# A two-block transformer kernel on one core: where the weight splits stand at the ends of the mixers and of the feed-forward layers

## The reference

```
for layer in range(2):
    u = rms_norm(h, g_mix[layer])
    h = h + mixer(u)                     # layer 0: MLA 8 heads | stick-breaking 8 heads; layer 1: chunk-band, 16 heads
    u = rms_norm(h, g_ffn[layer])
    h = h + (silu(u @ w_gate) * (u @ w_up)) @ w_down          # 1024 -> 2816 -> 1024
x = rms_norm(h, g_final)
```

## Time and profile before

| | |
|---|---|
| median of 3 runs | 1011.17 us (1009.79 to 1012.47) |
| the profiled execution | 1009.69 us |
| its span, first to last instruction | 1007.9 us |
| TensorE busy | 984.0 us, 98% of the span |
| VectorE, ScalarE busy | 629.4 us and 594.7 us |
| granted TensorE clock, mean | 0.998 of full speed |
| chain that ended last | TensorE 91%, ScalarE 4%, VectorE 4% |

### The profile page before, as it was taken

The page is one execution under the profiler, slowest core; times in us unless marked ns, Lnnn a source line. Parts: engine busy times, 40 slices in busy tenths (PEclk is TensorE's granted clock), DMA queues, the critical chain, the costliest instruction groups (busy, mean ns, idle before and its releaser), DMA issues.

```text
span 1007.9 us, 13330 instructions
## 1 busy us (share of the span) xinstructions
PE 984.0 (98%) x4920; PEld 791.8 (79%) x4920; DVE 629.4 (62%) x782; ACT 594.7 (59%) x929; POOL 12.2 (1%) x22
## 2 busy tenths in 40 slices
PE   6999899999999999999999999999999998999998
PEld 5888688888887777788888887877777777778877
DVE  5676675555556765665555556866666666776654
ACT  6776564444445655465454545766767676867571
POOL 1000000000000000000000000000000000000000
PEclk9999999999999999999999999999999999999999
DMA  8536247756563543457757654646434334336551
GB/s 272 177 114 204 84 137 239 247 169 206 168 206 128 180 155 125 127 168 254 227 188 227 231 185 132 207 163 199 132 125 134 116 126 135 118 124 209 197 179 42
DMA packets 106041, 170.26 MB, mean 169 GB/s; under 512 B 3988, under 2 KB 65302, under 8 KB 106000
## 3 DMA queue, kind: packets, MB, share of 16 engines
q1 hardware_dynamic: 103360, 161.23, 48.6%
q0 software_dynamic: 2304, 8.37, 2.6%
q10 hardware_dynamic: 336, 0.10, 0.0%
HBM read 168.58 MB, written 1.11 MB: 168 GB/s over the span
## 4 chain that ended last, share of the span: by engine, by line
PE 91%; ACT 4%; DVE 4%; issue 1%; DMA 0%; ACTq 0%; DVEq 0%
PE acc L434 13%; PE acc L436 12%; PE acc L435 12%; PE acc L485 11%; PE pair_ps L436 7%; PE pair_ps L434 7%; PE pair_ps L435 7%; PE acc L536 3%; PE acc L713 3%; PE acc L630 2%; PE turn_ps L609 2%; PE pair_ps L597 1%; PE acc L577 1%; PE pair_ps L596 1%; PE turn_ps L503 1%
## 5 line engine op out<-in xcount | busy, mean ns | idle before, releaser
L1666 DVE TENSOR_TENSOR w_lo<-w_raw,w_hi 128x2048 fp32r<-128x2048 f32 (+2 forms) x155 | 345.5, 2231 | 133.4 <-ACT w_hi L1027 133.0
L1027 ACT ACTIVATE w_hi<-w_raw 128x2048 fp32r<-128x2048 f32 (+2 forms) x155 | 288.4, 1863 | 78.3 <-PE acc L436 35.5
L434 PE MATMUL acc<-w_hi,uT_hi 128*128 128x512 f32 (+3 forms) x552 | 221.4, 401 | 3.5 <-DVE w_lo L2093 3.0
L436 PE MATMUL acc<-w_hi,uT_lo 128*128 128x512 f32 (+3 forms) x552 | 212.5, 385 | 0.0
L435 PE MATMUL acc<-w_lo,uT_hi 128*128 128x512 f32 (+3 forms) x552 | 211.9, 384 | 0.0
L434 PEld LDWEIGHTS acc<-w_hi,uT_hi 128*128 128x128 f32 x552 | 104.0, 188 | 30.9 <-issue 9.0
L434 PE MATMUL pair_ps<-w_hi,uT_hi 128*128 128x512 f32 x320 | 126.5, 395 | 0.0
L436 PE MATMUL pair_ps<-w_hi,uT_lo 128*128 128x512 f32 x320 | 124.8, 390 | 0.0
L435 PE MATMUL pair_ps<-w_lo,uT_hi 128*128 128x512 f32 x320 | 124.6, 389 | 0.0
L436 PEld LDWEIGHTS acc<-w_hi,uT_lo 128*128 128x128 f32 x552 | 104.0, 188 | 21.2
L435 PEld LDWEIGHTS acc<-w_lo,uT_hi 128*128 128x128 f32 x552 | 104.3, 189 | 17.4
(11 more groups left out here) (230 smaller groups left out, 1230.9 us busy)
## 6 DMA issues: line engine op xcount, KB each, us to landing
w_raw<-in_w_in SPq DMA_DIRECT2D x46, 1024.0 KB
w_raw<-in_w_gate SPq DMA_DIRECT2D x44, 512.0 KB
w_raw<-in_w_up SPq DMA_DIRECT2D x44, 512.0 KB
w_raw<-in_w_down SPq DMA_DIRECT2D x22, 1024.0 KB
w_raw<-in_w_out SPq DMA_DIRECT2D x12, 1024.0 KB
w_raw<-in_w_qkv SPq DMA_DIRECT2D x16, 512.0 KB
w_raw<-in_w_branch SPq DMA_DIRECT2D x6, 1024.0 KB
bias<-rel_rows POOLq DMA_DIRECT2D x5, 1024.0 KB, 7.9
```

The source lines that it names most:

```text
L434: mm(o, xh, wh[:, k, :], start=first and k == 0, stop=False)
L436: done = mm(o, xl, wh[:, k, :], start=False, stop=last and k == len(kts) - 1)
L1027: activation(w_hi[:, slot, 0:width], w_raw[:, slot, 0:width], ACT.Copy).then_inc(hi_done, 1)
L1666: v.tensor_tensor(w_lo[:, slot, 0:width], w_raw[:, slot, 0:width], w_hi[:, slot, 0:width].bitcast(f32), ALU.subtract).then_inc(lo_done, 1)
```

## The change

Only the order of calls is changed; no instruction of the computation is added or taken away.

- In the first mixer TensorE transposes the weights of pair 1 between the two column halves of the projection piece `(1, 1)`, and runs `values` of pairs 0 and 1 behind it, one after the other. The piece `(2, 1)` is cut in halves too, with `values` of pair 3 between them. ScalarE copies the turned weights of pairs 0 and 1 before the exponentials of pairs 2 and 3, and has its two `slot_step`s together behind `copy_probs(2)`. VectorE has its first `slot_step` behind `copy_probs(2)` and `normalise(3)` and its second behind the last `outputs`.
- In the band mixer VectorE computes `outs(0)` before `norm(3)`. The `slot_step` between `probs(4)` and `tops(6)` goes, and one more stands at the end: each of the four last units is split one place later.
- At the end of both feed-forward layers VectorE's last `slot_step` stands behind `split_hidden` of the last chunk.

```
--- TensorE, first mixer
                 logits("mla", 3, 4, 8)
-                out_piece(1, 1).then_inc(unit_used, 1)
-                turn_probs_and_values(0)        # values(t), then turn_probs(t + 1)
-                turn_probs_and_values(1)
+                out_piece(1, 1, (0,))
+                turn_probs("mla", 1, 4)
+                out_piece(1, 1, (1,)).then_inc(unit_used, 1)
+                pe.wait_ge(logit_read, 8)
+                values("mla", 0, 4)
+                values("mla", 1, 4)
+                turn_probs("mla", 2, 4)
                 pe.wait_ge(out_read, 6)
                 out_piece(2, 0)
-                turn_probs_and_values(2)
-                out_piece(2, 1).then_inc(unit_used, 1)
+                values("mla", 2, 4)
+                turn_probs("mla", 3, 4)
+                out_piece(2, 1, (0,))
                 values("mla", 3, 4)
+                out_piece(2, 1, (1,)).then_inc(unit_used, 1)
                 n.pair = 8
                 pe.wait_ge(out_read, 8)
                 closing_unit(2, 3, FFN0)
--- ScalarE, first mixer
                 exponentiate("mla", 1, 4, 0)
+                copy_probs(0, 4)
                 exponentiate("mla", 2, 4, 0)
-                copy_probs(0, 4)
-                slot_step()
+                copy_probs(1, 4)
                 exponentiate("mla", 3, 4, 0)
                 round_outputs("mla", 0, 4, 0)
-                copy_probs(1, 4)
                 round_outputs("mla", 1, 4, 0)
                 copy_probs(2, 4)
+                slot_step()
                 slot_step()
--- VectorE, band mixer
                 norm(2)
                 slot_step()
+                outs(0)
                 norm(3)
-                outs(0)
                 probs(2)
...
                 probs(4)
-                slot_step()
                 tops(6)
                 tops(7)
...
                 slot_step()
                 outs(7)
+                slot_step()
--- VectorE, first mixer
                 outputs("mla", 0, 4, 0)
-                slot_step()
+                outputs("mla", 1, 4, 0)
                 copy_probs(2, 4)
-                outputs("mla", 1, 4, 0)
                 normalise("mla", 3, 4)
                 slot_step()
                 copy_probs(3, 4)
                 outputs("mla", 2, 4, 0)
                 outputs("mla", 3, 4, 0)
+                slot_step()
--- VectorE, feed-forward
-                step(NF - 1)                    # slot_step, split_hidden, slot_step, gate, slot_step
+                slot_step()
+                split_hidden(NF - 2)
+                slot_step()
+                gate(NF - 1)
                 split_hidden(NF - 1, 2)
+                slot_step()
```

More of the change, by code:

```diff
@@ L828, in first_mixer @@
                 order = (4, 6, 0, 2)
[L830 to L835, removed]
                 def out_piece(i, blk, halves=(0, 1), first=False, last=False):
```

## The result

The changed kernel takes **1001.49 us** (median of 4 runs, 1001.39 to 1002.43); the kernel before, on the same chip, 1010.48 (4 runs, 1009.79 to 1012.47). The ratio is 0.9907, interval 0.9894 to 0.9921. The profiled execution took 1001.44 with a span of 999.7, against 1009.69 and 1007.9: 8.25 us less, where the forecast said 7.9. Median against median it is 9.0 less; that figure is not sharp, since two of the four runs before took 1009.79 and the other two 1011.17 and 1012.47, and their median lies in the gap.

The account below looks back on a forecast made before the run. TensorE, busy 98%, was taken to bound the kernel, leaving only its waits. Terms 4.2 + 2.1 + 0.3 + 1.3 = 7.9 us gave 1011.17 - 7.9 = 1003.3 us, own spread 1001.6 to 1005.2, range 1001.2 to 1006.6.

Parts of the forecast that it names:

- What bounds the kernel: Whole kernel: TensorE is busy 98%, so only its waits, some 20 us, can be won; won microseconds reach the end.
- Part 1: End of the first mixer: new orders bring the closing unit from 123.89 to 119.7, a gain of 4.2 us.
- at best all 4.33 that TensorE isn't busy: Upper bound for the first mixer's end: 18.95 us less 14.62 of TensorE's busy time.
- the sum's best case: All places together at their upper bounds: 4.3 + 2.2 + 1.7 = 8.2 us.
- Part 2: End of both feed-forward layers: VectorE's low part starts sooner, 1.04 us each, 2.1 together; first add covered by 0.1.
- Part 3: Band mixer: 0.3 us from `outs(0)` ahead of `norm(3)`, 1.3 from the split moved away ahead of `tops(6)`.
- Loads: SP's weight loads go out later, tightest at the second feed-forward layer's first unit with 10.2 us left; cost taken as nothing.
- The sum: Whole kernel: 4.2 + 2.1 + 0.3 + 1.3 = 7.9 us won, profiled execution from 1009.69 to 1001.8.
- The rule that was weighed: First mixer's end: headroom by the weight loads' busy share, giving 6.0 us there and a sum of 9.7; not adopted.
- Part of the waiting stays: Rival, 0.18: roundings or splits still delay `copy_probs(3)` or the first add; 4.9 us won, 1006.3.
- the gain doesn't reach the end: Rival, 0.08: a later stage is paced by other engines or loads; at most 3 us won, about 1010.
- Slower: Rival, 0.04: later loads land late at the second feed-forward layer's first unit; 1014 if landing takes 25 us.

Follow-up runs that it names:

- the repetition: The changed kernel run once more without an edit, for its spread: 1001.71 us (4 runs), ratio 0.9909 to the kernel before.

## Why the prediction was right or wrong

*What bounds the kernel* held: only TensorE's waits were to be had, and a microsecond won in one stretch was won at the end. The stages' differences add up to 8.25, and the two last layers took the same within 0.1.

*Part 1* was a little mis-sized: 4.54 instead of 4.2. The mechanism was right to the place, with a wait of 0.37 for `outputs(1)` (0.3 said) and `copy_probs(3)` 0.73 ahead of its use (0.8 said). The terms that were off: the half piece, put at 1.6 "plus 0.1 for its second start", took 1.57, 1.56, 1.57 and 1.50, together 0.2 less; four `values` took 3.05, not 3.2, since two in a row took 1.45; turns 1 and 3 took 0.57 and 0.63. With the rounding up of the sum that makes 14.41 where 14.8 was said. The bound "at best all 4.33 that TensorE isn't busy" was none: TensorE's busy time fell too, from 14.62 to 14.27. So the 8.25 won lies just above the sum's best case of 8.2.

*Part 2* held: 1.02 and 1.03 (1.04 said), with the cover of 0.1. The first feed-forward stage won 1.20; 0.13 of that comes with the first mixer's part alone, whose closing unit starts without a wait. *Part 3* held: 1.67 in the stage (0.3 + 1.3 said). The lead over the kernel before grew by 0.34 at `values(1)`, by 1.06 at `logits(7)` and by 0.3 up to the next piece. *Loads* held: in the timeline of the changed kernel ScalarE's rounding of the second feed-forward layer's first unit was released by TensorE's slot, not by a load:

```profile
405.33 0.37 SPq L266 DMA_DIRECT2D w_raw<-in_w_gate  x1
...
415.59 1.92 ACT L1026 ACTIVATE w_hi<-w_raw 128x2048 fp32r<-128x2048 f32 x1 [2.65 <-PE acc L713]
```

The 10.26 us between them are the 10.2 that was said.

*The sum* was 0.35 short: 1001.8 said for the profiled execution, 1001.44 measured. By stages, 0.21 of it lies in the first mixer (its end won 0.34 more, but began 0.13 later), 0.13 in the feed-forward layers, 0.07 in the band mixer, and 0.06 was lost behind them.

**The step that failed** is the last one: "the median of the runs lies 1.5 above it, so 1011.17 - 7.9 = 1003.3". It carries the 1.5 over to the changed kernel, as scatter that both kernels share. They do not share it: the runs of the changed kernel lie at the profiled time, their median 0.05 above it (1001.49 and 1001.44), and the four of the repetition with them. In the kernel before, 33 of 59 executions are 1.4 to 3.1 us longer than the profiled one. In two of the three profiles that have the wait of 2.46 (2.45 in one), TensorE's clock falls behind it, and filling the wait made the median 1.3 shorter. The change removes the wait, and the fall with it. So of the 1.8 by which the median is below the forecast, 0.35 is the sum and 1.45 this offset. That each of the 33 had the fall is not shown, since there are no traces of them, and in the longest a later start may add to it, as the 0.85 did with the feed-forward part alone.

The profile before could not show the fall, since the clock was 1.00 there; the three runs before, 1009.79, 1011.17 and 1012.47, spread by 2.7 and hinted at it. The same scatter, 1.4 to either side, made the forecast's own spread of 1001.6 to 1005.2. The median lies 0.1 below it; that it lies 0.3 above 1001.2, the lower end of the wider range, is no merit of the forecast, since the range was drawn that far for a rival.

*The rule that was weighed* said 6.0 for the first mixer's end, from a loads' busy share of 0.81. In the changed kernel's stretch TensorE is hardly ever without work; by the windows (span of the stretch, then busy PE, PEld, DVE, ACT, POOL):

```profile
105.07:119.48 14.41, 14.27 (x88) 10.51 (x87) 10.80 (x25) 9.52 (x23) 0.00 (x0) 1.00 0.18 59
```

The loads' share is 10.51 / 14.41 = 0.73, where the estimate took 0.81 from another stretch. By the windows of the same profile it is 0.74 in piece (2, 0) (2.18 of 2.95), 0.60 in `values(2)` (0.48 of 0.80) and 1.00 in turn 3 (0.63 of 0.63): it differs with the shape, as the prediction held against the estimate. The Trainium skill (Perfetto Trace Analysis, section Identifying the Most-Contended Engine) names this share, beside the share of peak arithmetic, as the measure of TensorE's headroom. Taken over from a stretch of other matmuls, it overstated the headroom here: 6.0 where 4.54 came.

*The rivals.* "Part of the waiting stays" and "the gain doesn't reach the end" fell with the waits list and the stages. "Slower" fell with the load's row. "More than the waits comes back" gave 1001.5, and that the median came out there is luck. Its sentence, that what starts behind a stall is slow at first, is true in the executions with the fall. In the profiled pair, where the clock was 1.00, it was worth at most the 0.35 by which TensorE was less busy: 4.54, not its 6.0. The rest of its 1.8 came from the offset, which it had not priced.

What stays open: why the clock falls behind the same wait in some executions and not in others, and for how long.

## What to carry to other kernels

Where one engine is busy 98%, list its waits, and look at what the releasing engine did just before: a long operation with a late due time ahead of a short one that is waited for can be a gain the size of the wait, and moving it costs nothing as long as it still ends before its own due time, which has to be worked out too. TensorE's order alone won 2.0 and the feeding engines' orders alone 1.7 of 4.54; the last 0.8 came only when both were changed. And runs that fall into groups are not mere scatter: before carrying an offset between profile and median over to the changed kernel, ask which wait could make it.

## What the runs showed of the hardware

A wait of 2.46 us, with one of 0.93 shortly ahead of it, let TensorE's granted clock fall from 1.00 to 0.50 in two of three profiles and not in the third, with the same code up to there. With nine idle matmuls in its place, executions beyond 1011 fell from 11 of 15 to 1 of 11, on the same chip.

In the profiles, much of the scatter that is left comes from the start. TensorE's matmuls at lines 434 to 436 follow one another by 0.43 us for the first microseconds, then by 0.23; the change comes at 14.6 us in the profile before, where the granted clock rises from 0.50 to 1.00, and at 17.3 with TensorE's order alone. In that second trace the record of the clock shows 1.00 from the start, though the matmuls follow one another by 0.43 as well, so the record can lack the low level. The matmul at line 775 so starts at 18.34 in the profile before, 18.43 with the change, 19.16 with the feed-forward part alone and 19.67 with TensorE's order alone, and the lag against the kernel before stays as it is up to the first mixer's end (0.8 and 1.4 us).
